# Sample differential attention moved from the last stage into the prompt's indexed attention, which then works in units of two heads

## The chip, the cores and the metric

The kernel runs on one core of a Trainium2 chip. The metric is the device time of one launch in microseconds (us), the median of the runs. One execution was also taken with the hardware profiler; its trace gives, per instruction, the engine, the start, the duration and what released it. TensorE is PE in the rows (PEld its weight loads), VectorE DVE, ScalarE ACT, GpSimd POOL, and SP issues DMA transfers only. A q behind a name (SPq, ACTq) means the time in which that engine's instruction queue issues a DMA.

## The reference, cut to what matters

Two layers of a decoder run for a prompt of 1024 rows and for a sample group of 8 sequences with 4 new rows each, which have 2048 past keys in paged caches. The change is in the second layer:

```python
qc, kc, vc, z_c, qd, kd, vd, qi, ki, wi, z_d = _split(h @ w_in, L1_SIZES)
# differential attention: two softmax maps, 4 heads of 2 x 64, values of 128
s = jnp.einsum('btghmd,bsgmd->btghms', qg, k) * scale
p = _masked_softmax(s, mask)
attn = p[..., 0, :] - lam * p[..., 1, :]
o = jnp.einsum('btghs,bsgd->btghd', attn, v)
# indexed attention: 8 heads over the 256 best keys of a row's index score
score = jnp.einsum('bth,bths->bts', wib * (IDX_HEADS ** -0.5), jax.nn.relu(idx_s))
top_s, top_i = lax.top_k(score, n_sel)
o = jnp.einsum('btghn,btngd->btghd', softmax(q @ k[top_i]), v[top_i])
y = concat(o_c * silu(z_c), o_d * silu(z_d)) @ w_out
x = x + gate * y            # and a last RMSNorm
```

Prompt rows take their keys from this launch, sample rows from the cached pages and their own 4 rows.

## The kernel before

It is a chain of stages, each a block with one hand-written instruction stream per engine, and a barrier between blocks. The last four matter here:

1. Prompt differential attention (`diff_prompt`).
2. `sample_index`: the index scores of the 32 sample rows over their 2048 past keys; POOL gathers the cached index keys.
3. `attend_pairs` for the prompt's indexed attention. A unit is one tile of 128 prompt rows with all 8 heads, two halves of 64 rows of the PE with four heads (`a` 0 to 3) each. For a unit the order (`attend_schedule`) has "scores" jobs (keys times queries into PSUM; the shifted scores and their peaks by DVE at L1285; exponentials by ACT at L1296; the division by the sum on POOL at L1467) and one "keys" step for each 128 keys: PE turns the weights (8 transposes, L1341), ACT copies the first half from PSUM (L1486), DVE the second (L1421), and PE multiplies them with the values one step behind (L1354). A tile i has i + 1 steps, so 36 in all. The next unit's scores jobs lie between a unit's steps.
   The same steps carry `SampleSearch`, the binary search for each sample row's 256th best score, in 33 looks, one to a step: DVE counts the scores over a threshold (L1897), PE adds the parts of a row (`add_parts`, L1894), DVE reads the total and sets the next bit.
4. `diff_dsa_sample_output`, the last stage: attention of the sample rows over their pages, units of `SampleAttention`, with the output projection (`OutputProjection`, 16 products "out" of 8 matmuls each, L2408) woven in. There are 8 units of differential attention (2 groups of sequences x 4 parts; `size` 2, that is 256 KB a transfer) and then 4 of indexed attention (`size` 1, 128 KB). A unit takes keys chunk by chunk (L2168), a softmax, turns (L2179) and values (L2193).

`SampleRing` holds the pages. A chunk is 8 transfers, one for each cached page pair, and each needs its page number read into a register of the issuing engine:

```python
for j in range(GB):
    for x in range(2):
        u = 2 * ((GB * group + j) * PAIRS + pair) + x
        rows = bass.ds(eng.value_load(k.page_list[0:1, u:u + 1]) * HD, HD)
        eng.dma_start(ring.both(n, j, slice(x * HD, (x + 1) * HD)), cache[rows, :]...
```

SP loads two chunks of three, ACT every third (`n % 3 == 2`), each once the slots of keys (`keyed`) and values (`freed`) that it takes are free.

Of the kernel before, what the change touches and what calls it, by code (L numbers as in the profile page):

```python
# [32 lines left out]
GB = 4  # L33
ROW = 512
PAIRS = PAST // (2 * P)
SAMPLE_UNITS = ((4, 9), (4, 10))
GROUPS = DB // GB
# [252 lines left out]
def dsa_tensors(k, st):  # L290

    k.sample_sel = k.sb(st, "dsa_mask_s", [NS, PAST + NS], BF16, side="right")
    k.sample = {n: k.sb(st, f"late_{n}", shape, side="right") for n, shape in (
        ("q", [P, 2, DB, 32]), ("q_new", [P, 1, DB, 32]), ("dsa_k", [P, NS]), ("dsa_v", [NS, P]))}
# [1005 lines left out]
def attend_pairs(k, name, units, base, blocks=None, between=None, search=None):  # L1300
# [7 lines left out]
    with ExitStack() as st:  # L1308
# [13 lines left out]
        out_banks = 2 if search is None else 1  # L1322
        out_bank = lambda u: k.bank[6 + units[u]["tile"] % out_banks]

        with nc.Block() as block:
            @block.tensor
            def _(pe):
# [16 lines left out]
                def values(u, s):  # L1344
# [4 lines left out]
                    if begin and i >= out_banks:  # L1349
                        pe.wait_ge(A.finished, i - out_banks + 1)  # L1350
# [8 lines left out]
                for what, u, x in A.order:  # L1359
# [4 lines left out]
                    if search:  # L1364
                        search.add_parts(pe)
# [6 lines left out]
            def _(dve):  # L1372
# [56 lines left out]
                if search:  # L1429
                    for _ in range(3):  # L1430
                        next(between)
                due, ended = [], []
                for e, (what, u, x) in enumerate(A.order):
                    while due and (e - due[0][0] >= 2 or (what == "keys" and due[0][1] == u)):
                        sums(*due.pop(0)[1:])
                    while ended and e - ended[0][0] >= 2 and not search:
                        finish(ended.pop(0)[1])
# [8 lines left out]
                    while ended and search:  # L1446
                        finish(ended.pop(0)[1])
# [395 lines left out]
def dsa_prompt(k):  # L1843

    with ExitStack() as st:
# [7 lines left out]
        for i in range(SEQ // P):  # L1853
            n = (i + 1) * P
            units.append(dict(tile=i, n=n, first=0, branch=None, steps=n // P, jobs=score_jobs([*range(4)], n), v=k.v["dsa"],
                              mask=sel[:, starts[i]:starts[i] + n], head=heads_of(i)))

        with ExitStack() as ws:
            sample_index(k, ws)
            search = SampleSearch(k, ws, k.qiT[0:NS, :, :].rearrange("p a n -> p (a n)"))  # L1860
            attend_pairs(k, "dsa", units, 4, None, chain(keep_dsa_sample(k, k.nc.vector), search.steps(k.nc.vector)), search)


class SampleSearch:
# [8 lines left out]
    def __init__(self, k, st, scratch):  # L1873
        self.k, self.scratch = k, scratch
        self.v = k.sb(st, "search_scores", [P, self.PART + NS])
        self.upper = k.sb(st, "search_upper", [P, self.PART + NS], BF16)
        self.upto = k.sb(st, "search_upto", [P, PAST + NS])
        self.ge = self.upto[:, :].bitcast(BF16)[:, 0:self.PART + NS]
# [6 lines left out]
        self.totalled = k.sem(st, "search_totalled")  # L1885
        self.total = k.bank[7][:, 0:1]
        self.counts, self.n = 33, 0

    def add_parts(self, pe):

        if self.n < self.counts:
            self.n += 1
            pe.wait_ge(self.counted, self.n)
            pe.matmul(self.total, self.same[:, :], self.seen[:, :], start=True, stop=True).then_inc(self.totalled, 1)  # L1894

    def count(self, dve, v, threshold, op):
        dve.tensor_scalar(self.ge, v, threshold, None, op, ALU.add, accum_out=self.seen[:, :]).then_inc(self.counted, 1)  # L1897

    def steps(self, dve):
        k, v, upper, found, tried, step = self.k, self.v, self.upper, self.found, self.tried, self.step  # L1900
        link = lambda ins: k.dve_order.link(dve, ins)
        score, m = k.sample_score, k.sample_sel
        link(dve.tensor_reduce(self.of_query[:, :], k.const("ident").rearrange("p (x n) -> p n x", n=NS), X, ALU.add))
        dve.tensor_copy(self.same[:, :].rearrange("p (x n) -> p x n", n=NS), self.of_query[:, :].unsqueeze(1).to_broadcast([P, P // NS, NS]))
        dve.memset(v[0:3 * NS, self.PART:], TAKEN)
        for j in range(4):
            last = dve.tensor_copy(v[NS * j:NS * (j + 1), 0:self.PART], score[:, self.PART * j:self.PART * (j + 1)])
# [1297 lines left out]
```

## Time and profile before

| | us |
|---|---|
| median of 3 runs | 2084.7 |
| lowest and highest | 2082.84 and 2085.32 |
| the profiled execution | 2079.67 |
| its span, first to last instruction | 2077.9 |
| mean granted PE clock, as a share of full speed | 0.906 |
| PE, DVE, ACT busy | 1692.5, 1066.2, 510.1 |

The trace's stages: the prompt's indexed attention runs from 1595.6 to 1746 us, the last stage from there to the end. Layer 0's last stage, from 739 to 928 us, has the same 16 products and 128 page transfers of 128 KB, and is quoted for comparison. PE's busy time is modelled from its pipelined matmuls, so a full PE still has some room.

### The profile page before, as it was taken

What the parts mean: (1) busy time and instruction counts of PE and PEld (TensorE: products, weight loads), DVE (VectorE), ACT (ScalarE), POOL (GpSimd) and SP (SyncE); (2) the same over time, 40 slices, a digit from 0 to 9 for tenths busy, and PEclk for the clock granted to TensorE, in tenths of its full rate; (3) what the DMA queues carried; (4) which work ended last, traced back from release to release, by engine and by line L of the source; (5) the groups of instructions that cost most, each with busy time, mean ns of one, the idle gap of its engine ahead of it and who ended that gap; (6) DMA issues with size and microseconds to landing.
All of it is one profiled execution on the core that took longest, in us unless ns stands there. A gap on an engine that the chain in (4) does not pass through costs nothing. (4 is left out here: it accounts for less than half of the span.)

```text
span 2077.9 us, 27607 instructions
## 1 busy us (share of the span) xinstructions
PE 1692.5 (81%) x10319; PEld 1026.2 (49%) x10319; DVE 1066.2 (51%) x2625; ACT 510.1 (25%) x1098; POOL 264.1 (13%) x358
## 2 busy tenths in 40 slices
PE   3599999956999987975999899985856895486766
PEld 2477666533445433545665566653553442243443
DVE  3113772187767632233049899916764885021323
ACT  3100001066555500003111001014533651010122
POOL 0111120002544300000000000002103430000000
PEclk9799999977999997997999999997987997598878
DMA  6521450071000076611111101100002003989672
GB/s 263 221 71 55 171 194 21 2 279 52 1 1 1 1 255 166 178 57 48 52 45 40 42 33 42 42 0 0 1 1 82 1 1 92 265 208 221 193 182 65
DMA packets 85910, 189.33 MB, mean 91 GB/s; under 512 B 11558, under 2 KB 48524, under 8 KB 78289
## 3 DMA queue, kind: packets, MB, share of 16 engines
q1 hardware_dynamic: 58032, 120.13, 18.8%
q0 software_dynamic: 10464, 46.45, 6.3%
q10 hardware_dynamic: 17280, 20.98, 4.2%
q8 instruction: 82, 1.34, 0.3%
q14 instruction: 52, 0.42, 0.1%
HBM read 172.57 MB, written 19.12 MB: 92 GB/s over the span
## 5 line engine op out<-in xcount | busy, mean ns | idle before, releaser
L846 PE MATMUL banks<-hT,w_in 128*128 128x352 f32 x1632 | 485.9, 460 | 3.9 <-ACT mix L974 3.9
L846 PEld LDWEIGHTS banks<-hT,w_in 128*128 128x128 f32 x1632 | 310.7, 191 | 176.4 <-ACT mix L974 4.4
L842 PE MATMUL banks<-w_in,hT 128*128 128x264 f32 (+5 forms) x1008 | 225.7, 380 | 18.7 <-DMA w_in<-in_w_in 18.7
L2408 PE MATMUL banks<-w_out,mix 128*128 128x512 f32 x512 | 235.4, 617 | 2.4 <-DVE sel_mask L2711 1.7
L842 PEld LDWEIGHTS banks<-w_in,hT 128*128 128x128 f32 (+1 forms) x1008 | 176.5, 189 | 56.5 <-DMA w_in<-in_w_in 19.2
L2408 PEld LDWEIGHTS banks<-w_out,mix 128*128 128x128 f32 x512 | 99.1, 198 | 124.6 <-issue 120.6
L2423 DVE TENSOR_TENSOR y<-banks,gate_rows 128x512 f32<-128x512 f32 x32 | 22.1, 692 | 230.7 <-PE banks L2408 230.7
L1467 POOL TENSOR_SCALAR nsa_p<-nsa_p,nsa_sum,gates 128x640 f32<-128x640 f32 (+7 forms) x128 | 100.4, 795 | 205.0 <-DVE nsa_sum L1407 205.0
L1296 ACT ACTIVATE nsa_p<-nsa_p,nsa_negmax 128x640 f32<-128x640 f32 (+7 forms) x128 | 92.6, 725 | 29.0 <-DVE nsa_negmax L1285 28.5
L1285 DVE CUSTOM_DVE_ANT_0 nsa_p<-banks,wide_masks 128x640 f32<-128x640 f32 (+7 forms) x128 | 84.0, 703 | 25.6 <-PE banks L1271 25.6
L1957 DVE TENSOR_SCALAR_CACHE_REDUCE dsa_mask<-mix,prompt_top_tried 128x384 bf16<-128x384 f32 (+5 forms) x96 | 85.9, 943 | 1.3 <-DVE kv_rows L906 0.2
L974 ACT ACTIVATE mix<-banks 128x352 f32<-128x352 f32 x48 | 22.0, 465 | 260.9 <-PE banks L846 239.1
L1957 DVE TENSOR_SCALAR_CACHE_REDUCE dsa_mask<-prompt_top_upper,prompt_top_tried 128x384 bf16<-128x384 bf16 (+5 forms) x90 | 80.8, 943 | 1.3
L1341 PE MATMUL banks<-cf,nsa_p 128*128 128x128 f32 x528 | 74.3, 283 | 8.4 <-POOL nsa_p L1467 5.5
L1341 PEld LDWEIGHTS banks<-cf,nsa_p 128*128 128x128 f32 x528 | 57.2, 142 | 38.6 <-ACT nsa_pT L1486 13.0
L2168 PE MATMUL banks<-ds_ring,diff_q 64*32 64x128 f32 x1024 | 23.6, 333 | 58.9 <-DMA ds_ring<-in_diff_pairs 58.8
L1605 POOL TENSOR_SCALAR diff_p<-diff_p,diff_sum 128x128 f32<-128x128 f32 (+7 forms) x32 | 24.5, 767 | 333.6 <-DVE diff_sum L1561 333.6
L1271 PE MATMUL banks<-dk_T,qcT 64*128 64x512 f32 (+3 forms) x192 | 43.0, 574 | 18.6 <-DVE diff_negmax L1285 17.8
L1467 POOL TENSOR_SCALAR dsa_p<-dsa_p,dsa_sum 128x128 f32<-128x128 f32 (+7 forms) x64 | 46.7, 745 | 86.8 <-DVE dsa_sum L1407 86.7
L1486 ACT ACTIVATE nsa_pT<-banks 128x512 f32<-128x512 f32 x66 | 39.0, 592 | 72.2 <-PE banks L1341 72.0
L1296 ACT ACTIVATE dsa_p<-dsa_p,dsa_negmax 128x128 f32<-128x128 f32 (+7 forms) x64 | 48.9, 766 | 16.2 <-DVE dsa_negmax L1285 15.9
L1538 PE MATMUL banks<-dv_v,diff_pT 128*128 128x128 f32 x288 | 41.4, 290 | 14.0 <-DVE diff_pT L1581 10.2
(522 smaller groups left out, 2347.3 us busy)
## 6 DMA issues: line engine op xcount, KB each, us to landing
w_in<-in_w_in SPq DMA_DIRECT2D x24, 1056.0 KB, 5.0
ds_ring<-in_diff_pairs SPq DMA_DIRECT2D x88, 256.0 KB, 6.7
ada_w<-in_l_ada_w SPq DMA_DIRECT2D x8, 1536.0 KB, 7.3
ns_ring<-in_sel_pairs SPq DMA_DIRECT2D x88, 128.0 KB, 2.9
ds_ring<-in_dsa_pairs SPq DMA_DIRECT2D x88, 128.0 KB, 3.4
ds_ring<-in_diff_pairs ACTq DMA_DIRECT2D x40, 256.0 KB, 10.0
ada_w<-in_l_ada_w SPq DMA_DIRECT2D x8, 1024.0 KB, 13.7
w_out<-in_l_w_out SPq DMA_DIRECT2D x4, 2048.0 KB, 16.5
```

The lines of the kernel that those rows point to most:

```text
L842: last = pe.matmul(bank[0:rows, 0:n], k.hT[:, a, r0:r0 + rows], w[:, j % slots, a, 0:n], start=(a == 0), stop=(a == KT - 1))
L846: last = pe.matmul(bank[:, 0:cn], w[:, j % slots, a, m * P:(m + 1) * P], k.hT[:, a, c0:c0 + cn], start=(a == 0), stop=(a == KT - 1))
L1271: last = pe.matmul(self.chain(c, half)[:, x * n + c0:x * n + c0 + cn], q, kT[:, c0:c0 + cn], start=True, stop=True, skip_group_check=True)
L1285: last = dve.tensor_tensor_reduce(self.p(u, h), self.chain(c, half)[:, x * n:(x + 1) * n], un["mask"], -1.0, 3e38, ALU.add, ALU.min, self. ...
L1296: last = act.activation(self.p(u, h), self.p(u, h), ACT.Exp, bias=self.nm[:, u, h:h + 1], scale=-1.0, accum_out=self.rs[:, u, h:h + 1])
L1341: last = pe.transpose(k.bank[4 + half][:, a * P:(a + 1) * P], src, k.const("ident"))
L1467: last = pool.tensor_scalar(A.p(u, h), A.p(u, h), A.rs[:, u, h:h + 1], gate, ALU.mult, ALU.mult)
L1486: act.activation(A.pT[:, g % 2, 0:512], k.bank[4][:, :], ACT.Copy).then_inc(A.copied[0], 1)
L1538: last = pe.matmul(out_bank(u)[:, a * P:(a + 1) * P], A.pT[:, g % 2, a * P:(a + 1) * P], k.v["dv"][:, s, (a // 2) * P:(a // 2 + 1) * P], s ...
L1605: last = pool.tensor_scalar(A.p(u, a), A.p(u, a), A.rs[:, u, a:a + 1], 1.0, ALU.mult, ALU.mult)
L1957: last = dve.tensor_scalar(m, v, threshold(j), None, op, ALU.add, accum_out=seen[:, j:j + 1])
L2408: last = pe.matmul(k.bank[u % 2][0:n, :], k.mix[:, a, r0:r0 + n], self.w[:, a, h * 512:(h + 1) * 512], start=a == 0, stop=a == KT - 1)
```

## The change

The 8 differential units leave the last stage. They run in a new block, `attend_indexed`, which replaces `attend_pairs` for the prompt's indexed attention, with a ring of their own (`MAP_UNITS`, 4 slots for keys and 6 for values, so two chunks of keys and three of values). Prompt units become half as wide: one tile and two of the four `a`, so that PSUM bank 7 and half of banks 4 and 5 come free. There are 16 units and 72 steps. The looks of the search are at two steps of three from step 6 on. A differential unit u starts at step 2 + 8u.

```diff
+MAP_UNITS = (4, 6)
@@ dsa_prompt
-            units.append(dict(tile=i, n=n, first=0, branch=None, steps=n // P, jobs=score_jobs([*range(4)], n), v=k.v["dsa"],
-                              mask=sel[:, starts[i]:starts[i] + n], head=heads_of(i)))
+            for a in (0, 2):
+                units.append(dict(tile=i, n=n, a=a, steps=n // P, jobs=score_jobs([a, a + 1], n), mask=sel[:, starts[i]:starts[i] + n], head=heads_of(i)))
+        sample = [dict(blocks=4, size=2, q=k.diff_q, q_new=k.diff_q_new, width=2 * P, new_mask=k.tailb[:, :], group=g, part=x, parts=4, pairs=2,
+                       transfers=2 * GB, load=load_pages(k, k.t["diff_pairs"]), new=x // 3,
+                       k_new=[k.diff_k_new[:, y, :] for y in range(2)], v_new=k.diff_v_new[:, :], finish=put)
+                  for g in range(GROUPS) for x in range(4)]
+        ring = SampleRing(k, st, "maps", sample, *MAP_UNITS, 2 * NS)
         with ExitStack() as ws:
-            sample_index(k, ws)
-            search = SampleSearch(k, ws, k.qiT[0:NS, :, :].rearrange("p a n -> p (a n)"))
-            attend_pairs(k, "dsa", units, 4, None, chain(keep_dsa_sample(k, k.nc.vector), search.steps(k.nc.vector)), search)
+            sample_index(k, ws, ring)
+        attend_indexed(k, units, 4, SampleMaps(k, st, ring), keep_dsa_sample(k, k.nc.vector), SampleSearch(k, st))
@@ SampleMaps.values
+        for c in range(2):
+            _, values = R.wait(pe, u, c)
+            for t in range(2):
+                i = 2 * c + t
+                for j in range(GB):
+                    last = pe.matmul(self.sum_bank[self.rows_of(j), 0:w], self.pT[:, i * P + 32 * j:i * P + 32 * (j + 1)],
+                                     values[:, j, t * w:(t + 1) * w], start=i == 0, stop=not un["new"] and i == 3, skip_group_check=True)
+            last.then_inc(R.freed, 1)
@@ indexed_order
+    base = attend_schedule(units)
+    steps = sum(1 for e in base if e[0] == "keys")
+    period = (steps - 8) / len(maps.units)
+    for u, un in enumerate(maps.units):
+        at = int(2 + u * period)
+        for n, what in ((0, "map_keys"), (1, "map_exp"), (3, "map_turn"), (4, "map_values"), (6, "map_end")):
+            due.setdefault(at + n, []).append((what, u, 0))
@@ with_map_loads
+    due = {n: ring.release[n] for n in range(2, len(ring.chunks)) if n % 3 == 2}
+        for n in [n for n, (a, b) in due.items() if a <= keyed and b <= freed]:
+            out.append(("map_load", n, 0))
@@ attend_indexed
+        looks = [g for g in range(6, len(step_at)) if g % 3 < 2][:search.COUNTS]
+            @block.sync
+                for n in range(2, len(M.R.chunks)):
+                    if n % 3 != 2:
+                        M.R.load(sp, n)
+                def turn(u, s):
+                    for half in range(2):
+                        if g:
+                            pe.wait_ge(copied[half], g)
+                        if half and g in look_at:
+                            search.add_parts(pe, look_at[g])
+                        for x in range(2):
+                            last = pe.transpose(k.bank[4 + half][:, x * P:(x + 1) * P], of(u, half, a + x)[0][:, s * P:(s + 1) * P], k.const("ident"))
+            # PE, before a step's turn, after a map's turn
+                        if map_turned is not None:
+                            M.banks_read(pe, map_turned)
+            # DVE at a step
+                        dve.wait_ge(turned, 2 * g + 2)
+                        if g in look_at:
+                            search.read(dve, look_at[g])
+                        copy(u, x)
+                        if g in look_at:
+                            search.go_on(dve, look_at[g])
+            # ACT
+                    elif what == "map_load":
+                        M.R.load(act, u)
+                    elif what == "map_turn":
+                        M.copy(act, u)
@@ diff_dsa_sample_output
-        units = [dict(blocks=4, size=2, q=k.diff_q, q_new=k.diff_q_new, width=2 * P, new_mask=k.tailb[:, :], group=g, part=x, parts=4, pairs=2,
...
-        units += [dict(blocks=2, size=1, q=s["q"], q_new=s["q_new"], width=P, new_mask=sel[:, PAST:PAST + NS], group=g, part=h, parts=2, pairs=4,
+        units = [dict(blocks=2, size=1, q=s["q"], q_new=s["q_new"], width=P, new_mask=sel[:, PAST:PAST + NS], group=g, part=h, parts=2, pairs=4,
-        order = mix_early(order, last_diff)
+        order = [("diff", 0), ("diff", 1), ("diff", 2)] + order
@@ sample_index
+            @block.sync
+            def _(sp):
+                sp.wait_ge(turned, 8)
+                for n in range(2):
+                    ring.load(sp, n)
```

Before, PE's rows in two late steps of the prompt's indexed attention (`dsa_pT` are the turned weights, `qdT` the queries, `search_seen` the counts):

```order
L1341 MATMUL banks<-cf,dsa_p 128x128 x8
L1894 MATMUL banks<-search_seen,search_same_query 128x1
L1354 MATMUL banks<-dsa_pT,dsa_v 64x512 x2
L1271 MATMUL banks<-dsa_T,qdT 128x512 x2
L1271 MATMUL banks<-dsa_T,qdT 128x256 x2
L1341 MATMUL banks<-cf,dsa_p 128x128 x8
L1894 MATMUL banks<-search_seen,search_same_query 128x1
L1354 MATMUL banks<-dsa_pT,dsa_v 64x512 x2
```

PE's rows in the same place with the change, three steps, the last behind the keys of a differential unit (`maps_ring` holds its pages):

```order
L2170 MATMUL banks<-cf,dsa_p 128x128 x2
L2360 MATMUL banks<-search_seen,search_same_query 128x1
L2170 MATMUL banks<-cf,dsa_p 128x128 x2
L2181 MATMUL banks<-dsa_pT,dsa_v 64x256 x2
L2170 MATMUL banks<-cf,dsa_p 128x128 x2
L2360 MATMUL banks<-search_seen,search_same_query 128x1
L2170 MATMUL banks<-cf,dsa_p 128x128 x2
L2181 MATMUL banks<-dsa_pT,dsa_v 64x256 x2
L1924 MATMUL banks<-maps_ring,diff_q 32x128 x64
L2170 MATMUL banks<-cf,dsa_p 128x128 x2
```

A step is half as wide, the sum of the counts stands between its two halves, and the keys of a differential unit, 64 matmuls, lie between two steps.

In the last stage PE's rows began, before, with the first differential units:

```order
L2168 MATMUL banks<-ds_ring,diff_q 32x128 x64
L2179 MATMUL banks<-cf,ds_p 128x128 x4
L2193 MATMUL banks<-ds_ring,ds_pT 32x256 x16
L2168 MATMUL banks<-ds_ring,diff_q 32x128 x64
L2408 MATMUL banks<-w_out,mix 128x512 x8
```

and with the change, at the same place, with the indexed ones (`late_q`):

```order
L2650 MATMUL banks<-ds_ring,late_q 32x128 x64
L2661 MATMUL banks<-cf,ds_p 128x128 x8
L2675 MATMUL banks<-ds_ring,ds_pT 32x128 x32
L2631 MATMUL banks<-dsa_mask_s,spreadb 128x32
L2634 MATMUL banks<-late_dsa_k,late_q_new 32x32 x4
L2643 MATMUL banks<-dsa_mask_s,spreadb 128x512 x2
L2650 MATMUL banks<-ds_ring,late_q 32x128 x32
L2890 MATMUL banks<-w_out,mix 128x512 x8
```

The first product (L2890, before L2408) now stands behind one whole indexed unit and two chunks of the next.

## Rows read from the trace of the kernel before

**Rows 1.** Busy time by stage: stretch, its us, each engine, PE clock, DMA share, GB/s.

```profile
739.00:928.00 189.00, 165.18 (x1462) 83.40 (x1462) 50.23 (x150) 12.78 (x30) 4.36 (x8) 0.90 0.59 179
1595.60:1746.00 150.40, 123.45 (x690) 66.53 (x690) 129.39 (x384) 72.28 (x165) 46.73 (x64) 0.94 0.00 1
1746.00:2078.00 332.00, 214.69 (x2552) 113.98 (x2552) 78.09 (x214) 43.78 (x79) 10.21 (x19) 0.79 0.76 192
```

**Rows 2.** The page: the chain that ended last, shares of the span by line.

```profile
SPq L2070 4%; DMA ds_ring<-in_diff_pairs 3%; PE banks L2408 2%; SPq L2069 2%; PE banks L2168 1%; ACTq L2070 0%; PE banks L2193 0%; DMA ds_ring<-in_dsa_pairs 0%; ACTq L2069 0%; PE banks L2179 0%; DVE x_tiles L2482 0%; PE banks L2435 0%; ACT L2474 0%; DVE y L2423 0%; DVE x_tiles L2426 0%
```

**Rows 3.** Timeline of SP's queue in the last stage: start, us, DMAs issued.

```profile
1763.42 5.53 SPq L2336 DMA_DIRECT2D w_out<-in_l_w_out  x2
1777.76 147.99 SPq L2070 DMA_DIRECT2D ds_ring<-in_diff_pairs  x72
1937.71 103.33 SPq L2070 DMA_DIRECT2D ds_ring<-in_dsa_pairs  x88
```

**Rows 4.** Groups of instructions in the last stage: busy us, mean ns, idle before.

```profile
L2168 PE MATMUL banks<-ds_ring,diff_q 64*32 64x128 f32 x1024 | 23.6, 333 | 58.9 <-DMA ds_ring<-in_diff_pairs 58.8
```

**Rows 5.** DMA issues: count, KB each, median us from issue to landing.

```profile
ds_ring<-in_dsa_pairs SPq DMA_DIRECT2D x88, 128.0 KB, 3.4
```

**Rows 6.** The chain in order of time, last stage: start, us, what.

```profile
1823.53 13.93 PE banks L2408 x32
1838.63 1.93 PE banks L2193 x32
...
1840.94 1.12 PE banks L2168 x64
```

**Rows 7.** Timeline of PE around the last product.

```profile
2044.49 7.13 PE L2408 MATMUL banks<-w_out,mix 128*128 128x512 f32 x16
```

**Rows 8.** Timeline of DVE in one late step of the indexed attention.

```profile
1716.59 0.15 DVE L1919 TENSOR_SCALAR search_step<-banks 128x1 int32<-128x1 f32 x1
...
1717.16 0.78 DVE L1897 TENSOR_SCALAR_CACHE_REDUCE search_upto<-search_scores,search_tried 128x544 bf16<-128x544 f32 x1
...
1718.30 0.69 DVE L1421 COPY dsa_pT<-banks 128x512 f32<-128x512 f32 x1 [0.35 <-PE banks L1341]
```

**Rows 9.** Timeline of PE in the same step.

```profile
1716.08 1.08 PE L1354 MATMUL banks<-dsa_pT,dsa_v 128*64 128x512 f32 x4
1717.09 1.10 PE L1341 MATMUL banks<-cf,dsa_p 128*128 128x128 f32 x8
1718.03 0.36 PE L1894 MATMUL banks<-search_seen,search_same_query 128*128 128x1 f32 x2
```

**Rows 10.** Timeline of DVE, a copy of half the width.

```profile
1755.24 0.42 DVE L2392 COPY gate_rows_s<-banks 128x256 f32<-128x256 f32 x1 [8.11 <-PE banks L2385]
```

**Rows 11.** Timeline of PE over a step with a scores job.

```profile
1678.52 1.09 PE L1341 MATMUL banks<-cf,dsa_p 128*128 128x128 f32 x8
...
1680.80 1.77 PE L1271 MATMUL banks<-dsa_T,qdT 64*128 64x512 f32 x8
1682.51 0.66 PE L1341 MATMUL banks<-cf,dsa_p 128*128 128x128 f32 x4
```

**Rows 12.** Groups by shape in the indexed attention.

```profile
L1285 DVE CUSTOM_DVE_ANT_0 dsa_p<-banks,dsa_mask 128x896 f32<-128x896 f32 x8 | 8.4, 1085 | 1.1 <-PE banks L1271 1.1
```

**Rows 13.** Timeline of ACT and DVE in a differential unit, last stage.

```profile
1768.89 7.71 ACTq L2070 DMA_DIRECT2D ds_ring<-in_diff_pairs  x8
...
1777.32 0.42 DVE L2228 CUSTOM_DVE_ANT_0 ds_p<-banks,wide_masks 128x256 f32<-128x256 f32 x1 [19.26 <-PE banks L2168]
...
1780.34 0.60 ACT L2287 ACTIVATE ds_pT<-banks 128x512 f32<-128x512 f32 x1 [1.21 <-PE banks L2179]
```

**Rows 14.** Busy time in parts of the indexed attention, columns as in rows 1.

```profile
1595.60:1614.40 18.80, 11.35 (x55) 7.78 (x55) 14.45 (x71) 10.48 (x39) 6.46 (x16) 0.64 0.00 1
1614.40:1729.30 114.90, 103.57 (x596) 55.28 (x596) 101.17 (x307) 60.01 (x124) 40.27 (x48) 1.00 0.00 1
1729.30:1746.00 16.70, 8.53 (x42) 3.47 (x40) 13.78 (x9) 1.79 (x3) 0.00 (x0) 0.89 0.00 0
```

More of the change, by code:

```diff
@@ L1297, in exponentials, with attend_pairs @@
         last.then_inc(self.exped, 1)
-def attend_pairs(k, name, units, base, blocks=None, between=None, search=None):
+def attend_pairs(k, name, units, base, blocks=None, between=None):
     nc = k.nc
@@ L1435, in _ @@
                         sums(*due.pop(0)[1:])
-                    while ended and e - ended[0][0] >= 2 and not search:
+                    while ended and e - ended[0][0] >= 2:
                         finish(ended.pop(0)[1])
@@ new lines, in indexed_order @@
+def indexed_order(units, maps):
+    base = attend_schedule(units)
+    steps = sum(1 for e in base if e[0] == "keys")
+    period = (steps - 8) / len(maps.units)
+    due = {}
+    for u, un in enumerate(maps.units):
+        at = int(2 + u * period)
+        for n, what in ((0, "map_keys"), (1, "map_exp"), (3, "map_turn"), (4, "map_values"), (6, "map_end")):
+            due.setdefault(at + n, []).append((what, u, 0))
+        if un["new"]:
+            due.setdefault(at + 7, []).append(("map_join", u, 0))
+    order, g = [], 0
+    for e in base:
+        if e[0] == "keys":
+            order += due.pop(g, [])
+            g += 1
+        order.append(e)
+    for g in sorted(due):
+        order += due[g]
+    return order
@@ L1921, in steps, with read @@
-        kth = found[:, :].bitcast(F32)
-        self.count(dve, v[:, :], kth, ALU.is_gt)
+    def read(self, dve, n):
+        link = lambda ins: self.k.dve_order.link(dve, ins)
+        if n == 0:
+            link(dve.tensor_scalar(self.found[:, :], self.total, float(TOPK), -1.0, ALU.is_lt, ALU.mult))
+        elif n < self.COUNTS - 1:
+            link(dve.tensor_scalar(self.step[:, :], self.total, float(TOPK), float(1 << (31 - n)), ALU.is_ge, ALU.mult))
+        else:
+            link(dve.tensor_scalar(self.need[:, :], self.total[0:NS], -1.0, float(TOPK), ALU.mult, ALU.add))
@@ L1932, in steps @@
[L1932 removed]
+        link(dve.scalar_tensor_tensor(m[:, :], score, kth, equal, ALU.is_lt, ALU.add))
+        yield
         link(dve.tensor_scalar(m[:, :], m[:, :], NEG, None, ALU.mult))
@@ L2711, in vector @@
             dve.tensor_copy(self.selT[:, :, :].rearrange("p g n -> p (g n)"), k.bank[5][0:32, 0:GROUPS * P]).then_inc(self.read, 1)
-def mix_early(order, last_unit):
-    ends = [x for x, e in enumerate(order) if e[0] == "end" and e[1] == last_unit][0]
-    tiles = [x for x, e in enumerate(order) if e[0] == "out" and x > ends][:2]
-    out = list(order[:ends + 1]) + [("diff", 0)]
-    for x in range(ends + 1, len(order)):
-        out.append(order[x])
-        if x in tiles:
-            out.append(("diff", 1 + tiles.index(x)))
-    return out
 def nsa_sample_output(k):
```

456 lines of the change are left out of this document (399 added, 57 removed).

## The prediction

> **What bounds the kernel now.** I read the busy times by stage first, because the change touches two stages only. The last stage takes 332 us and PE is busy for 215 of them, at a mean granted clock of 0.79; the prompt's indexed attention takes 150 us, and there both PE (123) and DVE (129) are nearly full while DMA moves nothing [rows 1]. The chain that ended last says what the last stage waits for: its heaviest link is SP's queue at L2070, the page issues, then the landing of differential pages, and the products at L2408 only third [rows 2]. SP's own timeline shows why: 72 issues took 148 us, 88 more 103 us [rows 3], and 8 issues on ACT 7.7 us [rows 13]. So a transfer costs its queue about 1.0 us whatever its size, and a chunk of 8 about 8. PE waited 58.9 us for differential pages in front of their keys [rows 4].
>
> So the last stage is held by the pages and has about 117 us without PE work; the attention before it is held by DVE and PE together. The change brings work from the one to the other.
>
> **The last stage afterwards.** It keeps 16 products, 4 indexed units and 128 transfers of 128 KB. I walk through it. Before the first product stand one unit and two chunks (order rows). SP issues 16 pages (16 us), w_out (5.5) [rows 3] and 8 pages more (8), which land 3.4 us after issue [rows 5]: 33 us. That unit's softmax, turns and values take some 9, the next keys 1; chunks 0 to 5, w_out and the first x tiles are together 12 MB, 46 us at the pace of the differential chunks (2.1 MB in 8 us). First product at 46. Then 16 products at 6.97 [rows 6] are 112; three units at 6.2 (keys and values half as dear as a differential unit's, below, but four chunks) are 19; softmax waits that nothing covers, 3 a unit, 9. The end behind the last product was 2077.9 − 2051.6 = 26 us [rows 7]; the last unit's join no longer lies in it, so 24. Sum 210, rounded to 212 for waits at chunks 6 and 7. As a check, layer 0's like stage takes 189 us [rows 1]; it has no final norm behind its last product and starts its products sooner, so 212 stands in a fair place above it. The last stage gives back 332 − 212 = 120 us. SP's 88 issues (89 us) no longer bind it.
>
> **The indexed attention afterwards.** The same prompt heads in twice as many steps, 72, plus 8 differential units. Full-clock PE work per differential unit: keys 2 x 1.12, values 2 x 1.93 [rows 6], turns and new rows 0.5: 6.6 us, so 53 in all. DVE has 2 x 0.42 for the shifted scores [rows 13], 0.42 for the raw sums and small pieces, 2.4 with the joins, 19 in all. Splitting 36 copies of 0.69 [rows 8] into 72 of 0.42 [rows 10] adds 5.4 us of DVE.
>
> The Trainium skill, "Perfetto Trace Analysis", section Optimizing Scalar/DVE Operations, says that each DVE operation pays a fixed data access, some 125 ns from PSUM, and that larger operations are better on a full engine; by its figure the 36 extra copies would cost an estimated 4.5 us. The rows agree within a microsecond.
>
> Work alone would give PE 123 + 53 = 176 and DVE 129 + 19 + 5 = 154. But I expect the chain through a look to set the step, since its count now stands between the halves of a turn. In late steps, from the start of the count: 0.84 us until PE begins to add (1717.16 to 1718.00), 0.3 for the addition, two transposes 0.4 (half of a half of 1.10), 0.1 to DVE, read 0.15 and its fence 0.04, copy 0.35, two small operations 0.4: 2.55 us from look to look [rows 8, 9]. Over a step without a look it is 2.95, because DVE's copy must come before PE's second half. Three steps take 5.5 us; in work they have 3.4 (PE). From step 6 to 54 that makes 16⅓ x 5.5 = 90 us.
>
> On this chain fall, step by step:
> - The start: three wide steps took 18.8 us [rows 14]; six narrow ones with the first map keys, 22.
> - Scores jobs: at 896 columns PE 1.77 [rows 11] and then DVE 2 x 1.0 [rows 12]. PE's part hides behind the count, most of DVE's does not: +1.95 a job. Before, the same job turned 2.2 us into 3.99 (1678.52 to 1682.51) [rows 11], +1.8. By width 0.5, 0.7, 1.1, 1.5, 1.95, 2.3, four jobs each and the small tiles: 34.
> - Differential units: keys 2.24 on PE and 1.15 on DVE behind them, +1.7; exponential +0.3; the turn, +0.6, as PE must see the 0.60 copy [rows 13] before it may write bank 4 again; values 3.9, +2.7 after the slack of a look; raw sums +0.7; joins +0.8. 6.8 x 8 = 54.
> - ACT's chunks 2, 5, 8, 11 and 14: 7.7 us of issue each [rows 13], in which no step's first half is copied; PE stops after one step. After keys +4, after values (5 and 11) +4.8: 22.
> - The end: 17 steps without looks at 1.1 (PE 1.09, halves of rows 9), 19; the search's last operations, which held the last three steps to 16.7 us [rows 14], now one to a step, +9.
> - Where a map's PE piece meets a job's DVE piece one hides the other: −8.
>
> Sum 90 + 22 + 34 + 54 + 22 + 28 − 8 = 242. The same way of adding gives 33 x 2.2 + 34 + 19 + 17 = 143 for the 150 us of before, so it does not overstate. In front, SP's first two chunks (4 MB, behind the eighth turn of sample_index) compete with the last gathers of index keys: 0 (they have landed) to 10 (they halve in speed); I take 4, nearer to the first as only five are left.
>
> Are the pages in time? The second chunk of a unit is free to load at the first values of the unit before, four steps ahead of its keys: 8 issues and 3.4 to 5 us of landing, 12 us; four steps at 242/72 are 13.4. Just in time, 0. Early steps may wait 1 or 2.
>
> On ACT's part a rule of the Trainium skill speaks against the change: "DMA: Bandwidth & Descriptors", Rules for kernel authors, says that spreading DMAs over issuing engines brings no bandwidth, all run on the same 16 engines, and saves only issue time. The trace agrees that issue time is what a queue has too little of in the last stage, but in 242 us SP alone could issue all 128 pages (130 us). By the rule ACT's share buys nothing here, and its 22 us would be a pure loss; the sum keeps them as a cost either way.
>
> **Sum.** −120 + (242 − 150) + 4 = −24 us, against the profiled 2079.7: 2056. The median of the runs lies 5.0 above that execution; 2084.7 − 24 = 2061.
>
> **The rivals.**
> 1. Forecast: the look chain and the pieces that fall on it set the attention stage, 225 to 262 us. Chance 0.5. Result 2044 to 2081.
> 2. The pieces hide well, and the stage is held by PE's work at the ratio of before (123/150): 176/0.86, that is 205, and half of ACT's pauses, 11: 216. Total −120 + 66 + 4 = −50: 2035. For it speaks that PE and DVE were 90% and 88% busy in the middle 115 us [rows 14]; against it, that a wide step had 2.2 us of PE work to lay over the count and a narrow one has 1.1. Chance 0.25.
> 3. Slower: nothing hides. PE works its list in order, and behind the wait for a count stand the second half, the values, the scores and the map's keys; if each piece falls on the chain with its PE and its DVE price, a unit costs 9.5 instead of 6.8 (+22), a job 1.2 more (+30): 294, total −120 + 144 + 4 = +28: 2113. It decides from an attention stage of 266 us on, 3.7 us a step. For it speaks that a map's scores can be read only when all its keys are through; against it, the +1.8 a job measured before. Chance 0.19, most of it near the lower end.
> 4. The relief does not come: w_out and pages share the queues at the start and the last stage stays near 240. Then +4, 2088. The 117 us without PE work speak against it. Chance 0.06.
>
> **Numbers.** A change within 0.2%, 4 us, can't be told from none by a measurement of this kernel. Case 1 lies on the faster side for all but a tenth, case 2 wholly; cases 3 and 4 are the slower side but for a part within the 4 us. Faster 0.73, same 0.07, slower 0.20. The range runs from 2030 (case 2 with its full hiding) to 2095 (the nearer half of case 3); case 1's own is 2044 to 2081.
>
> **What would show it.** The last stage at 205 to 220 us, first product 44 to 50 us in, PE over 85% busy behind it. In the attention, steps at 3.3 us on average, two looks apart 2.5 us where no job falls, PE and DVE both at 65 to 75%, ACT's queue in five blocks of 8 us with PE waiting for ACT's copy of `dsa_pT` after each. Waits of PE for `maps_ring` under 10 us in total. The forecast is wrong if the last stage takes over 230 us, if steps take over 3.7 us (case 3) or under 3.0 (case 2), or if map pages come late.

## The result, and the profile after

The changed kernel takes 2130.7 us (median of 4 runs, 2126.5 to 2134.8), the kernel before 2083.8 (2080.1 to 2085.3): a ratio of 1.0228, 95% interval 1.0203 to 1.0253. It is 47 us slower; the forecast was 2061. The profiled execution is the slowest of its four (2134.8), and that of before (2079.7) is faster than all four listed, so the traces lie 55 us apart. 10 of these have gathered before sample_index begins (1560.1 against 1570.0), in stages that the change doesn't touch; in the traces of the experiments below it begins between 1563.7 and 1571.5.

Busy time of the changed kernel by stretch, columns as in [rows 1]: sample_index, the attention up to the first look, the looks, the steps behind them, the last stage.

```profile
1570.00:1612.10 42.10, 26.73 (x162) 13.05 (x162) 10.67 (x34) 9.43 (x16) 15.24 (x16) 0.72 0.83 199
1612.10:1640.20 28.10, 14.35 (x196) 8.64 (x196) 13.45 (x67) 10.50 (x39) 6.56 (x16) 0.77 0.30 76
1640.20:1854.30 214.10, 150.82 (x1606) 79.20 (x1602) 111.90 (x382) 63.96 (x158) 35.85 (x44) 0.81 0.48 119
1854.30:1918.70 64.40, 48.23 (x402) 23.35 (x400) 31.99 (x61) 14.09 (x34) 5.40 (x4) 0.75 0.14 34
1918.70:2133.00 214.30, 158.11 (x1188) 75.34 (x1188) 57.85 (x130) 28.98 (x49) 10.20 (x19) 0.85 0.48 139
```

The last stage is what it was forecast to be, 214 us for 212. The attention is not: 307 us for 242, against 150 before [rows 1]. Its clock is lower in each part than the 0.94 of before, and neither PE nor DVE is as full as there.

Waits of the changed kernel in the attention stage (engine, line, for what: us, times, longest):

```profile
ACT dsa_pT L2306 <- PE banks L2170: 128.3, 50, 12.5
DVE dsa_sum L2227 <- ACT dsa_p L2298: 54.1, 20, 9.7
ACT dsa_pT L2306 <- issue: 50.1, 5, 12.6
...
PE banks L2170 <- ACT dsa_pT L2306: 31.9, 7, 6.8
DVE dsa_p L2220 <- PE banks L2156: 27.5, 18, 3.7
DVE search_step L2385 <- PE banks L2170: 25.6, 15, 8.1
```

Two of these the forecast did not have, or not in this size: DVE waits 54 us for ACT's exponentials before it takes reciprocals (L2227), and ACT's five blocks of page issues hold it 50 us. Around one of the five, ACT, DVE and PE by their timelines:

```profile
1722.93 7.71 ACTq L2552 DMA_DIRECT2D maps_ring<-in_diff_pairs  x8
1730.74 0.38 ACT L2306 ACTIVATE dsa_pT<-banks 128x256 f32<-128x256 f32 x1 [12.55 <-issue]
1731.02 0.93 ACT L2298 ACTIVATE dsa_p<-dsa_p,dsa_negmax 128x768 f32<-128x768 f32 x1
...
1732.99 0.17 DVE L2227 RECIPROCAL dsa_sum<-dsa_sum 128x2 f32<-128x2 f32 x1 [8.32 <-ACT dsa_p L2298]
...
1731.18 0.69 PE L2170 MATMUL banks<-cf,dsa_p 128*128 128x128 f32 x2 [6.71 <-ACT dsa_pT L2306]
```

Of ACT's 12.55 us only 7.71 are issues. The load first waits 4.7 us for the map's keys, which PE ends at 1723; a copy and two exponentials stand behind it. DVE stops for the exponentials, PE for the copy. PE's granted clock in steps of 4 us, the same place:

```profile
1724.00:1728.00 4.00, 0.47 (x4) 1.00 0.75 201
1728.00:1732.00 4.00, 0.69 (x2) 0.68 1.02 243
1732.00:1736.00 4.00, 2.45 (x10) 0.50 0.38 80
1736.00:1740.00 4.00, 3.65 (x15) 0.50 0.00 0
1740.00:1744.00 4.00, 3.46 (x12) 0.50 0.02 4
1744.00:1748.00 4.00, 4.00 (x42) 0.69 0.00 0
```

The clock falls at about 1729, while PE is idle. After 6.7 idle us PE works at 0.50, 1.2 instead of 2.4 GHz, until about 1746. Two halves of values take 1.12 us there instead of 0.65, a scores job of 128x768 2.93 instead of 1.56. The Trainium skill, "TensorE: Matmul & The Clock Gate", section Part 1: The HAM clock gate, says that an idle array falls to 1.2 GHz; the trace agrees.

The other wait, on DVE and ACT at a job with a map entry behind it:

```profile
1707.49 0.17 DVE L2227 RECIPROCAL dsa_sum<-dsa_sum 128x2 f32<-128x2 f32 x1 [2.16 <-ACT dsa_p L2298]
1707.57 0.14 DVE L2385 TENSOR_SCALAR search_step<-banks 128x1 int32<-128x1 f32 x1
...
1705.46 0.38 ACT L2306 ACTIVATE dsa_pT<-banks 128x256 f32<-128x256 f32 x1 [0.53 <-PE banks L2170]
1705.74 0.82 ACT L2298 ACTIVATE dsa_p<-dsa_p,dsa_negmax 128x640 f32<-128x640 f32 x1
```

PE had added the count by 1705.6, but DVE reads it at 1707.57: the reciprocal stands ahead of it and waits for exponentials that ACT has behind its copy. The rule in the code is "two entries of the order later". With map entries in the order, two entries no longer span a step.

### The profile page after: what moved, and what is told of

Read it like the earlier page. It is cut to its first block and busy times, and to the rows that moved or that the text cites. A ratio compares the mean times of both kernels' runs of the same rounds, so it can differ in the third digit from the quotient of the medians.

```text
span 2133.0 us, 28145 instructions
## 1 busy us (share of the span) xinstructions
PE 1733.2 (81%) x10463; PEld 1033.8 (48%) x10463; DVE 1073.8 (50%) x2666; ACT 512.1 (24%) x1134; POOL 265.2 (12%) x358
## 5 line engine op out<-in xcount | busy, mean ns | idle before, releaser
L2890 PE MATMUL banks<-w_out,mix 128*128 128x512 f32 x512 | 230.4, 606 | 1.7 <-DVE sel_mask L3193 1.7
L2890 PEld LDWEIGHTS banks<-w_out,mix 128*128 128x128 f32 x512 | 97.1, 194 | 120.5 <-issue 117.9
L2170 PE MATMUL banks<-cf,dsa_p 128*128 128x128 f32 x288 | 66.0, 339 | 54.1 <-ACT dsa_pT L2306 31.9
L2170 PEld LDWEIGHTS banks<-cf,dsa_p 128*128 128x128 f32 x288 | 38.6, 177 | 89.9 <-ACT dsa_pT L2306 38.7
L2306 ACT ACTIVATE dsa_pT<-banks 128x256 f32<-128x256 f32 x72 | 27.3, 380 | 178.6 <-PE banks L2170 128.3
L2220 DVE CUSTOM_DVE_ANT_0 dsa_p<-banks,dsa_mask 128x128 f32<-128x128 f32 (+7 forms) x64 | 45.4, 753 | 27.5 <-PE banks L2156 27.5
```

The costliest lines, as they stand in the source:

```text
L2170: last = pe.transpose(k.bank[4 + half][:, x * P:(x + 1) * P], of(u, half, a + x)[0][:, s * P:(s + 1) * P], k.const("ident"))
L2220: dve.tensor_tensor_reduce(dst, chain(c)[half][:, x * n:(x + 1) * n], un["mask"], -1.0, 3e38, ALU.add, ALU.min, peak).then_inc(read, 1)
L2890: last = pe.matmul(k.bank[u % 2][0:n, :], k.mix[:, a, r0:r0 + n], self.w[:, a, h * 512:(h + 1) * 512], start=a == 0, stop=a == KT - 1)
```

## The experiments

All stretches below are read from the runs' traces as above: sample_index from DVE's first operation of it, the attention from PE's first scores product to the end of the last product with `mix`, the last stage from there to the end. Each stretch is of one execution, and that can lie some us beside its run's median: that of e4_both is 6.5 us below it, that of e2_late_sums 5.4 above. Ratios are of medians, to the kernel before in the same batch. Batches ran on different chips.

| run | sample_index | attention | last | ratio (95%) |
|---|---|---|---|---|
| before | 36 | 150 | 332 | 1 |
| changed | 42 | 307 | 214 | 1.0228 (1.0203–1.0253) |
| e1_sp_loads | 41 | 276 | 214 | 1.0065 (1.0040–1.0091) |
| e2_late_sums | 39 | 290 | 214 | 1.0102 (1.0058–1.0146) |
| e4_both | 41 | 254 | 213 | 0.9974 (0.9954–0.9994) |
| e3_no_maps | 33 | 209 | 215 | 0.9694 (0.9652–0.9735) |
| e9_narrow_no_looks | 33 | 167 | 215 | 0.9517 (0.9495–0.9539) |
| e10_wide_no_looks | 33 | 135 | 336 | 0.9934 (0.9907–0.9960) |
| e5_scores_in_look | 42 | 271 | 217 | 1.0025 (1.0005–1.0046) |
| e6_filler | 41 | 253 | 213 | 0.9956 (0.9936–0.9976) |
| e7_first_late | 48 | 262 | 213 | 1.0009 (0.9985–1.0033) |
| e12_first_in_attention | 33 | 271 | 215 | 1.0010 (0.9990–1.0030) |
| e8_spread_looks | 41 | 240 | 224 | 0.9939 (0.9918–0.9961) |
| e11_looks_off_jobs | 41 | 268 | 213 | 1.0032 (1.0012–1.0051) |
| e14_mixed_looks | 39 | 254 | 215 | 0.9951 (0.9932–0.9970) |
| e13_maxima_behind | 42 | 284 | 215 | 1.0101 (1.0081–1.0121) |
| e15_behind_and_mixed | 41 | 285 | 213 | 1.0109 (1.0084–1.0134) |

**ACT's pages (e1).** All chunks on SP, none in the order:

```
-    due = {n: ring.release[n] for n in range(2, len(ring.chunks)) if n % 3 == 2}
+    due = {}
-                    if n % 3 != 2:
-                        M.R.load(sp, n)
+                    M.R.load(sp, n)
```

> All 128 map pages on SP's queue, none on ACT's. Theory A: each of the five blocks of 7.7 us on ACT's queue stops the exponentials and the copies queued behind it, DVE then waits for them (8.3 us at 1725) and PE for DVE and ACT (6.7 us), and PE comes back at a granted clock that is lower for some 17 us; 9 to 11 us each, so the time falls by 45 to 55 us, to about 2080, and the granted clock of the attention stage rises. Theory B, the prediction's price: 22 us for the five, 2109. Theory C, the step is held by the chain through the looks and the pauses only fill it: 5 to 10 us, 2123.

The stage is 31 us shorter, and the ratio falls by 0.0163, 34 us: between A and B. A overstated it: DVE still waits 30 us for ACT's exponentials, of the 54. C is out.

**The reciprocals (e2), and both (e4).** The rule counts steps, no longer entries:

```
-                    while due and (e - due[0][0] >= 2 or (what == "keys" and due[0][1] == u)):
+                    while due and (passed > due[0][0] or (what == "keys" and due[0][1] == u)):
...
-                        due.append((e, u, x))
+                        due.append((passed, u, x))
...
+                        passed += 1
```

> DVE's reciprocals of the row sums come after the next step's look and copy, as in the kernel before, and no longer before it when a map entry stands between. DVE waited 54 us for ACT's exponentials in 20 pieces, some 35 of them in the five blocks of page issues on ACT's queue. Theory A: about 14 reciprocals stand ahead of a look that ACT's exponentials of 1 to 2 us hold up; 12 to 20 us less, 2113. Theory C, the chain through the looks waits there anyway, for PE's turn behind the map's values: under 5 us.

> Pages on SP alone and the reciprocals behind the look. Theory A: the two add up but for what they share (the 35 us of DVE waiting in ACT's blocks count once): 55 to 65 us less than the changed kernel, 2070, below the kernel before (2084). Theory B: 22 + 12, 2097. Theory C: under 15 in all, 2118.

17 us in the stage alone (A's 12 to 20; by the ratios the whole gains 26), 21 on top of e1 (276 to 254; 19 by the ratios). Together 52 us: not quite A's 55 to 65. The changed kernel with both is 0.26% below the kernel before. PE waits of e4 in the stage:

```profile
PE banks L2360 <- DVE search_ge L2363: 12.6, 8, 3.7
PE banks L2169 <- POOL dsa_p L2288: 8.1, 6, 3.5
PE banks L2169 <- ACT dsa_pT L2306: 5.4, 5, 2.2
...
PE banks L1924 <- DMA maps_ring<-in_diff_pairs: 4.6, 3, 1.7
```

Even with all 128 transfers on one queue (16 in sample_index, 112 here), pages hold PE for only 4.6 us. Its wait for ACT's copies falls from 31.9 to 5.4, and the stage's granted clock rises from 0.79 to 0.89.

**The split alone (e3), and without looks (e9, e10).** In e3 and e9 the map entries are filtered out of the order, SP loads none of their pages, and the sample's differential rows are a constant; e9 has no `look_at` either, e10 is the kernel before with `counts` at 0, both with a constant for the sample's threshold.

```
-    return order
+    return [e for e in order if e[0] in ("scores", "keys")]
```

> The indexed attention in units of two heads alone: the 8 map units, their 128 pages and their joins are left out (the sample's differential rows are set to a constant), the last stage is as in the changed kernel. The prediction's sum without its map and page terms is 90 + 22 + 34 + 28 = 174 us for the attention stage; with sample_index back at 35 us the time is 2131 - 133 - 7 = 1991. If the split itself costs more than was thought (every half falls on the chain), the stage takes 200 or more and the time is above 2015. If it costs nothing beyond DVE's 5 us, 155 and 1972.

> Units of two heads, no map units and no pages (as in the run without map units: attention stage 209 us, whole 2024), and besides the 33 looks of the sample's search left out (no count, no read, no addition; the sample's threshold is a constant). Theory A, the split costs because a step of half the width has not enough work to lay over the look's chain: without looks the stage is held by PE's 112 us of work and takes 125 to 140, the whole 1940 to 1955, with a granted clock near 1.0. Theory K, the halves themselves cost (72 times the passage from a turn through the copies to the values): the stage stays over 165, the whole over 1980.

> The kernel before with the 33 looks left out in the same way (attention stage 150 us with them, PE 123 us busy, 10.7 of them the additions). Theory A: a wide step covers the chain, so little comes of it: PE's 112 us and the waits for jobs, stage 120 to 135, whole 2055 to 2070. If the looks cost as much here as in narrow steps (60 us or more), the split is not what made them dear.

The same prompt heads take 150 us wide and 209 narrow; without looks 135 and 167. So the split costs 59 us: 32 of itself, 27 more through the looks (42 narrow, 15 wide). Theory A of e9 (125 to 140) is wrong; theory K (over 165) named the outcome. e10 comes out at the upper end of its A. The three attention stages e3, e9 and e10, as windows:

```profile
1599.10:1808.40 209.30, 163.74 (x834) 79.25 (x834) 142.19 (x430) 77.52 (x201) 49.95 (x64) 0.82 0.00 1
```

```profile
1600.70:1767.70 167.00, 137.30 (x768) 65.14 (x768) 101.21 (x271) 77.61 (x201) 49.97 (x64) 0.90 0.00 1
```

```profile
1597.10:1732.40 135.30, 114.65 (x624) 55.63 (x624) 93.39 (x225) 71.50 (x165) 46.91 (x64) 0.95 0.00 1
```

Clocks of 0.82, 0.90 and 0.95 are 75, 33 and 14 us at the lower level ((1 − clock) / 0.5 of the stage). With PE busy all that time each such us would cost half of one. So at most 10 of the 32 us, and at most 21 of the 42, are the clock's; it follows the waits and adds to them.

The same rows divide the 32 us between e10 and e9: PE is idle for 29.7 us instead of 20.7, and busy for 137.3 instead of 114.7. Of the 23 us of busy time some 8 are the clock's (PE's busy stretches, each weighted with its granted clock, come to 124.8 and 110.5 us), and 14 are the same products done in smaller pieces. Single rows give an estimate of that size: a wide turn and its values take 1.10 + 1.08 us [rows 9], two narrow ones 2 x (0.66 + 0.65), 0.44 more for each of the 36 wide steps, 16 us. The ends of matmuls are modelled, so this is rough. The prediction let the split add to DVE's work only.

What a look costs with a job on the way is read from a job of 896 columns in e3, DVE first, then PE:

```profile
1704.96 0.78 DVE L2362 TENSOR_SCALAR_CACHE_REDUCE search_ge<-search_scores,search_tried 128x544 bf16<-128x544 f32 x1
...
1705.68 0.42 DVE L2231 COPY dsa_pT<-banks 128x256 f32<-128x256 f32 x1
1709.05 1.09 DVE L2218 CUSTOM_DVE_ANT_0 dsa_p<-banks,dsa_mask 128x896 f32<-128x896 f32 x1 [2.95 <-PE banks L2154]
...
1711.08 0.15 DVE L2384 TENSOR_SCALAR search_step<-banks 128x1 int32<-128x1 f32 x1
```

```profile
1704.53 1.11 PE L2168 MATMUL banks<-cf,dsa_p 128*128 128x128 f32 x4
1705.57 1.12 PE L2179 MATMUL banks<-dsa_pT,dsa_v 128*64 128x256 f32 x4
1706.62 2.38 PE L2154 MATMUL banks<-dsa_T,qdT 64*128 64x512 f32 x8
```

From this count to the next are 7.35 us (1712.31), the job's products 2.38 and its maxima 2.03 one behind the other, while the count itself hides 0.8. The clock is at the lower level for the first part of it; at the full one these products take 1.77.

In e9, at the same width and full clock, PE waits for the copy that stands behind the maxima:

```profile
1704.25 0.66 PE L2168 MATMUL banks<-cf,dsa_p 128*128 128x128 f32 x4
1704.84 0.65 PE L2179 MATMUL banks<-dsa_pT,dsa_v 128*64 128x256 f32 x4
1705.42 0.44 PE L2168 MATMUL banks<-cf,dsa_p 128*128 128x128 f32 x2
1706.87 0.44 PE L2168 MATMUL banks<-cf,dsa_p 128*128 128x128 f32 x2 [1.01 <-DVE dsa_pT L2231]
```

A wide step leaves 2.2 us of work on PE over the maxima (turn and values), a narrow one 1.2. But this is only part of the 32: PE waits for DVE's copies 18.5 us in 17 pieces in e9 and 8.1 in e10, so 10 us, and all of PE's idle time grows by 9. That the maxima are the cause of these 10 is argued from rows; e13 below didn't bear out a cure.

**Jobs (e5, e13).** e5 puts 12 jobs' products between the two halves of a look's turn (the diff's core; e4 else); e13 puts a job's maxima behind the next copy and ACT's exponentials a step later.

```
                     for half in range(2):
...
+                        if half and between is not None:
+                            scores(*between)
                         if half and g in look_at:
                             search.add_parts(pe, look_at[g])
```

> Pages on SP, reciprocals behind the look, and 12 of the 28 scores jobs put on PE between the two halves of a look's turn, where PE waits for DVE's count. Against the kernel with the two mends (2083, attention stage 254 us). In the kernel without map units a look behind a step without one took 3.6 us without a job and 5.8 with one, with 1.9 us of maxima on DVE. Theory D, a job falls on the chain with its products (1.6 us at full clock, 3 at half) and with its maxima: 12 x 1.2 to 1.6 us less, 2065 to 2068. Theory of the prediction, only DVE's part is on the chain and the products are hidden already: no gain, 2083, or some us more, because the addition is queued behind 1.6 us of products.

> The kernel with the two mends (attention stage 254 us), and a job's two maxima on DVE (2 us at 896 columns) behind the next step's look and copy, no longer ahead of them; ACT's exponentials of a job a step later too, behind the next copy. Theory L: in narrow steps PE starves while the maxima stand ahead of the copy (waits for DVE's copy of 18.5 us in 17 pieces without looks, 8 in the wide kernel); behind the copy PE has the values of two steps and a turn to do, 1.75 us instead of 1.2: 0.5 us on each of some 25 jobs, 10 to 15 us less, about 2070. Theory M, DVE's time between two copies is the same wherever the maxima stand, and ACT's later exponentials only move the wait: 0 to 10 us more, 2083 to 2093.

Both are slower, e5 by 16 us in the stage, e13 by 30, more than M allowed. Theory D is wrong as it was put: ahead of the turn, the products already run during the count, and moved they end some 0.4 us later (4.72 us behind the start of a count in e5, 4.35 at the same job in e4) and hold back the addition as well. For 12 jobs that is some 5 of the 16 us; the rest isn't traced, but the stage's clock is 0.84 instead of 0.89. Theory L in e13 fails too, by another resource, as PE's timeline shows:

```profile
1702.88 0.65 PE L2180 MATMUL banks<-dsa_pT,dsa_v 128*64 128x256 f32 x4
1705.54 0.70 PE L2155 MATMUL banks<-dsa_T,qdT 64*128 64x512 f32 x2 [2.01 <-DVE dsa_negmax L2219]
```

The next job's products need the banks that the delayed maxima still read. The edit moved ACT's exponentials as well, so it does not tell whether the maxima ahead of the copy make the 10 us.

**The clock (e6).** Two unread 128x128 products ahead of each `wait_ge(self.counted, n + 1)` on PE, else e4.

> The kernel with the two mends, and two idle products of 128x128 on PE ahead of each wait for a count (33 times), which nothing reads. Theory E, the granted clock falls because PE stands waiting, and the slow stretches cost: PE then shows a clock nearer to 1.0 in the attention stage (0.80 to 1.00 by part before) and the stage gets 10 to 20 us shorter, 2063 to 2073. Theory F, the clock is no cause of its own, PE is only early or late for the chain: 0 to 8 us longer, since each pair takes 0.4 us, 2083 to 2091.

The stage is 253 us for 254, and the clock between the first look and the last 0.94 for 0.92. The products cost nothing that can be seen, though PE is busy for 12 us more, so PE does wait there. But they hardly moved the clock, so neither E nor F is decided.

**The first pages (e7, e12).** `sp.wait_ge(turned, 8)` becomes 16 in e7; e12 has no load in sample_index and starts at chunk 0 in the attention. Both else e4.

> The kernel with the two mends, SP's first two chunks of map pages start when all 16 runs of index keys are turned, not 8. sample_index took 42 us in the changed kernel, 35.6 in the kernel before and 32.6 without the pages. Theory G, the pages take the gathers' bandwidth: sample_index falls back by 6 to 8 us; the first map keys come at the third step, some 7 us after the stage's start, the first chunks need 16 us of issue and 4 of landing, so PE waits 8 to 12 us for them there: 0 to +5 in all, 2083 to 2088.

> The kernel with the two mends, SP's first two chunks of map pages issued from the attention stage on, none within sample_index. In the run with the later start the block did not end before SP had issued them (47 us). Theory G, the pages take bandwidth from the gathers of index keys and nothing else is in play: sample_index falls from 41 to 33 to 36 us; the first map keys at the third step then wait for 16 us of issue and 4 of landing, some 10 us: 0 to +6 in all, 2083 to 2089.

e12 shows that the pages cost 8 us in sample_index, which falls from 41 to 33, as in e3. With them PE waits 9.8 us for the gathered keys instead of 6.0, and its clock there is 0.71 instead of 0.84; how the 8 divide between the two isn't shown. The attention gives back 16, more than the 10 expected: PE waits 12 us for pages, and 20 us near the start (1607 to 1627) pass at a clock of 0.59, where the first 20 of e4 have 0.92. In e7 SP issues the 16 pages from 1596.6 to 1612.5 and the block ends only then (47 us), which was overlooked. The early start is worth its price: the whole is no faster without it.

**Where the looks stand (e8, e11, e14, e15).** Only the list of steps with a look differs from e4:

```
+        looks = [g for g in range(6, len(step_at)) if g % 2 == 0][:search.COUNTS]                        # e8
+        looks = [g for g in range(6, len(step_at)) if g not in behind_job][:search.COUNTS]               # e11
+        looks = [g for g in range(6, len(step_at)) if (g % 2 == 0 if g < 42 else g % 3 < 2)][:search.COUNTS]   # e14
```

> The kernel with the two mends, the 33 looks at every second step (6 to 70) and no longer at two of three (6 to 54). Theory A, the chain through neighbouring looks sets the step: two looks apart by two steps need 2.9 us, as much as a look behind a step without one now, so the stage takes 33 x 2.9 + the same jobs and map pieces, and gains the 9 to 17 us of the end without looks, less 8 us of the search's last operations behind the last step: 5 to 15 less, 2068 to 2078. Theory H, what is between the looks (jobs, map pieces) sets the time and not their number in a row: within 5 us of 2083.

> The kernel with the two mends, and the looks only at steps with no scores job and no map keys right ahead, so that DVE never reads a count behind a job's maxima; the last look is near step 60 and no longer 54. With looks at every second step the stage was 240 us (254 without), but the search's end then stood behind the last step (+11). Theory A: 235 to 245 us for the stage without that end, the whole 2062 to 2072. Theory H, work between looks sets the time whatever their places: 254 and 2083.

> The kernel with the two mends, looks at every second step up to step 40 and at two of three from 42 to 63, so that the search's end still fits into the steps behind the last look. Theory A, what a look costs depends on the work since the last one: 18 of the looks lie apart as with every second step, which made the stage 14 us shorter, so 7 to 12 us less, 2071 to 2076. Theory H, only what lies between counts: 2083.

> Both edits. If both theories (L and A) hold, their gains add up but for a few us: 2060 to 2066. If only A holds, as the run with mixed looks plus what the moved maxima cost.

e8 comes out as A said, though by the traces with 14 us less in the stage and 11 of them given back, because the search's end now stands alone (DVE of e8):

```profile
1848.50 4.47 DVE L2408 TENSOR_TENSOR_SCAN maps_ring<-cf,maps_ring 32x2080 f32<-32x2080 f32 x1
1853.00 2.37 DVE L2410 SCALAR_TENSOR_TENSOR maps_ring<-maps_ring,search_need 32x2080 f32<-32x2080 f32 x1
1855.41 2.37 DVE L2412 SCALAR_TENSOR_TENSOR dsa_mask_s<-qiT,search_found,maps_ring 32x2080 bf16<-32x2080 f32 x1
```

e11, with looks in rows of two to four between jobs, has a stage 14 us longer than e4, outside both of its theories, so keeping looks away from jobs is no cure; that a count serves as cover for the job between two looks would fit, but isn't shown. e14 has the stage of e4 and a ratio 0.0023 lower, within both intervals: no gain shown. e15 is e13 again. The lowest ratio of the whole kernels is e8's, 0.6% below the kernel before (interval 0.9918 to 0.9961); e6 and e14 can't be told from it.

## Why the prediction was wrong

**The last stage: right in sum.** 214 us for 212. PE by the timeline at the first and at the last products:

```profile
1974.85 7.13 PE L2890 MATMUL banks<-w_out,mix 128*128 128x512 f32 x16
...
2096.72 14.64 PE L2890 MATMUL banks<-w_out,mix 128*128 128x512 f32 x32
```

The first product stands 56 us in, 10 later than the 46 of the forecast and outside its 44 to 50: PE waits 22.9 us for pages before it. From there to 2111.4 are 137 us for 16 x 6.97 + 19 + 9 = 140, and the end is 22 for 24. So 5 of the 10 were made up by terms taken too high, and 2 by the rounding from 210 to 212. PE is 96% busy behind the first product (over 85 said).

**The step that failed is the attention's sum, 242 for 307**, by three terms, and one that came out by luck.

- The base, "90 + 22 + 34 + 28" = 174, is 209 in e3. The start was right (21.6 for 22), and nearly so was the chain by itself: looks neighbouring each other with nothing between stand 2.51 us apart at best and 2.87 on average (forecast 2.55), across a step without one 2.85 at best and 3.56 on average (2.95). The jobs were not. The forecast let a job's products hide behind the count, but a count is 0.8 us, and values and products before the maxima are 3.4 in the step shown (2.4 at the full clock): across a step without a look and with one job on the way, 5.8 us on average for at most 4.9 by the sum. From the first count to the last, 144 us passed for 90 and some 27 of jobs; the 17 steps behind took 44 for 28 and some 6 of jobs, at a clock of 0.75, as DVE's scan stands in them. The intervals without a job are 5 of the 27 us that the looks took longer than forecast, those with one 22. The check against the wide kernel (143 for 150) proved little, since the price of a job, +1.8, had itself been read from the wide kernel.
- ACT's pauses, 22: 31 measured in the change (e1), 35 beside late reciprocals (254 in e4, 290 in e2). Priced was the issue alone. Left out were the load's wait for keys in front of it (4.7 us in the one shown), the exponentials behind it and the lower clock after it.
- The reciprocals, not priced at all: 17 to 21.
- The differential units: "54" less 8 of hiding, 46, for 45 measured (e4 against e3). This is luck. The prediction reads a unit's values as 2 x 1.93 us, but the 32 matmuls of 1.93 [rows 6] are the values of a whole unit (256 rows for 8 units in the trace of before). PE's work weighted with its clock grows by 38 us from e3 to e4, not by the 53 of the forecast. With 1.9 for the values, +0.7 instead of +2.7 behind the slack of 1.2, a unit is 4.8 and the sum 38 − 8 = 30 for the 45: the pieces fall on the chain for more than their price, and the doubled term made up for it.

In the order of the runs e3, e4, e2 and the change: 209 + 45 (map units) + 35 + 17 = 306, against 174 + 46 + 22 + 0.

**sample_index**: +6.5 in the traces, 8 by e12, within the 0 to 10, above the 4 taken.

**Pages just in time: right.** PE's wait for `maps_ring` is under 1 us with ACT's share and 4.6 without it.

**The rule on spreading DMAs** ("DMA: Bandwidth & Descriptors", Rules for kernel authors, of the Trainium skill): e1 agrees that ACT's share bought nothing (the stage is 276 us without it, 307 with it), and the pure loss was 31 us, more than the 22 written beside it.

**What would have shown it**: steps of 4.3 us on average (3.3 said, over 3.7 for rival 3), PE 70% busy between first and last look (65 to 75 said), DVE 52%, below the same range.

**The rivals.** Rival 3 named the outcome: slower, stage 294, +28. Its mechanism is half of it: the jobs lie on the chain, the map units cost 45 us, not 76, and the rest are the two couplings through ACT. Rival 2 fell with e3, rival 4 with the last stage. The two traces' −118 + 157 + 6.5 = +45, plus the 10 from upstream, make their 55.

What stays open is what makes PE wait in narrow steps (9 of the 32 us of the split without looks; the maxima ahead of the copy are argued, not shown), and how the 42 us of the looks divide between the waits and the clock that follows them.

## What to carry over

When a finer grain is laid into a chain of short hand-overs, price what each in-order engine has queued while it waits (a hand-over that a wide step covers with 2.2 us of work is bare at 1.2), and the added time of the same work in smaller pieces, on every engine. Never put a queue's waits and page issues on an engine whose copies and exponentials others wait for: five blocks of eight cost 31 us here, not the 22 of the forecast. And a lag counted in entries of an order changes its meaning when the order gets new kinds of entries; counting it in steps was worth 17 to 21 us here. A term that comes out right in size is no proof of its working: count the instructions of a row before its time is doubled.

## What the runs showed of the hardware

- The lower clock outlasts its cause: after 6.7 us without work PE stayed at 0.50 for over 12 us while 61 to 100% busy (1732 to 1746), so one pause is paid twice.
- A DMA issue with its page number read into a register costs ACT 0.96 us of its time (7.71 for 8) and SP 1.0 (15.95 for 16), and SP alone fed 112 transfers of 256 KB through the stage with 4.6 us of waiting by PE (e4), all 128 with 12.1 (e12).
- 4 MB of pages beside indirect gathers made the gathers' stage 8 us longer (41 in e4, 33 in e12).
- The same products in pieces of half the width kept PE busy for some 14 us more at equal clock (124.8 against 110.5, e9 and e10).
